# Mixer of a hybrid decoder layer: a step's instructions in another order on four queues

## What is computed

```
A  stick-breaking attention, 4 heads x 64      w = exp(z + suffix sums of log_sigmoid(-z)),  out = w @ v
B  gated delta rule, 4 heads x 128             m = strict_lower((k*beta) @ k^T * decay);  (1 + m)^-1 applied to values and keys
                                               v_new = u - w @ S;  o = (q*decay) @ S + (q @ k^T * decay) @ v_new
                                               S = S * chunk_decay + (k*decay)^T @ v_new
C  gated linear recurrence, 4 heads x 64       o = (q*exp(b)) @ S + scores(q, k, b) @ v;   S = exp(last)*S + (k*exp(last-b))^T @ v
mix = [rms(A)*gain, rms(B)*gain*silu(z), rms(C)*gain*sigmoid(g)];  x = x + mix @ w_out
x = x + (silu(h @ w_gate) * (h @ w_up)) @ w_down,  h = rms(x);   out = rms(x)
```

## Time and profile before

| | |
|---|---|
| TensorE busy | 1334.3 us, 96% of the span |
| DVE, ScalarE, POOL busy | 783.0, 591.8, 674.5 us |
| chain that ended last | PE 85%, DVE 4%, issue 4%, ACT 3%, POOL 2% |
| from 460 to 635 us, by windows of 25 us | TensorE busy 19.8 to 22.1 us, DVE 14.8 to 21.0, granted clock 0.86 to 0.93 |
| log_sigmoids (L1769), start and duration | 462.43: 0.42 us; 535.81: 1.10 us; 559.87: 1.11 us |
| softplus at 534.45 | three ACTIVATE, 1.33 us |
| out_high at 554.35 | 1.06 us |
| Exp of decays at 552.43 | 0.63 us |
| POOL's unit at 457.91, 128x256 | 0.71 us |
| two DVE products on update, 128x128, at 542.12 and 543.33 | 0.29 us each |

### The profile page before, as it was taken

The page is one execution under the profiler, slowest core; times in us unless marked ns, Lnnn a source line. Parts: engine busy times, 40 slices in busy tenths (PEclk is TensorE's granted clock), DMA queues, the critical chain, the costliest instruction groups (busy, mean ns, idle before and its releaser), DMA issues.

```text
span 1389.9 us, 24260 instructions
## 1 busy us (share of the span) xinstructions
PE 1334.3 (96%) x9101; PEld 1110.0 (80%) x9101; DVE 783.0 (56%) x1171; ACT 591.8 (43%) x1403; POOL 674.5 (49%) x583
## 2 busy tenths in 40 slices
PE   5999999999999888888999999999999999999997
PEld 4777887978888777777888788888888888788886
DVE  5014635557354588785147955555555556665657
ACT  6234535444343556552133433333333334344445
POOL 3233324143253577660210876766666777654442
PEclk9999999999999999898999999999999999999999
DMA  5131312423226333514210245444554545886663
GB/s 183 33 104 50 104 61 79 126 65 120 64 78 158 115 101 91 172 56 156 61 31 1 83 130 162 148 161 157 174 174 144 174 144 205 300 276 192 189 195 121
DMA packets 160371, 178.60 MB, mean 128 GB/s; under 512 B 9520, under 2 KB 110464, under 8 KB 160256
## 3 DMA queue, kind: packets, MB, share of 16 engines
q1 hardware_dynamic: 160112, 176.53, 40.1%
q10 hardware_dynamic: 144, 0.52, 0.1%
HBM read 124.32 MB, written 52.71 MB: 127 GB/s over the span
## 4 chain that ended last, share of the span: by engine, by line
PE 85%; DVE 4%; issue 4%; ACT 3%; POOL 2%; DMA 1%; SPq 0%; DVEq 0%; ACTq 0%; POOLq 0%
PE banks L2416 9%; PE banks L2417 9%; PE banks L2418 9%; PE banks L353 6%; PE banks L355 6%; PE banks L354 6%; PE banks L2427 4%; PE banks L2429 4%; PE banks L2428 4%; PE banks L692 2%; PE banks L693 2%; PE banks L694 2%; PE banks L2108 2%; PE banks L2110 2%; PE banks L2109 2%
## 5 line engine op out<-in xcount | busy, mean ns | idle before, releaser
L2574 POOL TENSOR_TENSOR w_l<-area,w_h 128x512 fp32r<-128x512 f32 x119 | 175.5, 1480 | 180.0 <-ACT w_h L2469 135.0
L2574 POOL TENSOR_TENSOR w_l<-w_raw,w_h 128x512 fp32r<-128x512 f32 x100 | 140.5, 1406 | 99.7 <-ACT w_h L2524 50.3
L353 PE MATMUL banks<-act_h,w_h 128*128 128x512 f32 x352 | 141.4, 402 | 0.0
L355 PE MATMUL banks<-act_h,w_l 128*128 128x512 f32 x352 | 137.5, 391 | 0.0
L354 PE MATMUL banks<-act_l,w_h 128*128 128x512 f32 x352 | 137.3, 390 | 0.0
L341 POOL TENSOR_TENSOR w_l<-w_raw,w_h 128x1024 fp32r<-128x1024 f32 x24 | 59.4, 2478 | 142.5 <-ACT w_h L334 125.3
L2416 PE MATMUL banks<-act_h,w_h 128*128 128x512 f32 x320 | 124.5, 389 | 0.0
L2417 PE MATMUL banks<-act_l,w_h 128*128 128x512 f32 x320 | 124.5, 389 | 0.0
L2418 PE MATMUL banks<-act_h,w_l 128*128 128x512 f32 x320 | 124.5, 389 | 0.0
L2427 PE MATMUL banks<-w_h,act_h 128*128 128x512 f32 x308 | 120.1, 390 | 0.3 <-DVE act_l L2726 0.3
L2428 PE MATMUL banks<-w_l,act_h 128*128 128x512 f32 x308 | 119.9, 389 | 0.0
(11 more groups left out here) (316 smaller groups left out, 3353.3 us busy)
## 6 DMA issues: line engine op xcount, KB each, us to landing
w_raw<-in_w_in SPq DMA_DIRECT2D x22, 512.0 KB, 4.1
w_raw<-in_w_gate SPq DMA_DIRECT2D x22, 512.0 KB, 4.6
area<-in_w_up SPq DMA_DIRECT2D x22, 512.0 KB, 4.8
ff_wide<-in_w_down SPq DMA_DIRECT2D x22, 512.0 KB, 4.4
down_sums<-ff_wide SPq DMA_DIRECT2D x11, 1024.0 KB, 4.1
area<-in_x SPq DMA_DIRECT2D x8, 1024.0 KB, 8.0
projected_tm<-area SPq DMA_DIRECT2D x32, 256.0 KB, 2.4
hidden_sums<-area SPq DMA_DIRECT2D x6, 1024.0 KB, 4.2
```

The costliest lines, as they stand in the source:

```text
L353: e.matmul(dst, w_h[:, b, k], act_h[:, k, cols], start=(k == 0), stop=False)
L355: mm = e.matmul(dst, w_l[:, b, k], act_h[:, k, cols], start=False, stop=(k == KT - 1))
L2574: e.tensor_tensor(slot(w_l, u), raw_use(u) if u < NU_FF else wd_raw(u - NU_FF), slot(w_h, u).bitcast(F32), ALU.subtract).then_inc(sems["fl ...
```

## The change

No instruction is added or taken away. These move within a step:

- TensorE: `key_key(v)` goes ahead of `gated_state(t)`.
- ScalarE: `decays` is split. Its first Exp (`decays`) goes behind `high(s, 1)`; the four Abs and the last Exp become `distances(v)` and go to the step's head. `softplus(u)` at the head becomes `softplus(v)` at the end of the step before. `inverse(u, 2)` goes ahead of `high(s, 0)`, `inverse(u, 4)` ahead of the last span.
- DVE: `log_sigmoids(u)` at the head becomes `log_sigmoids(v)` near the end of the step before. `final_sb(t)`, the scalings, become `final_sb(s)`, in the next step behind `gated_state(s)`. `update(u, 5)`, takes 6 and 7 go ahead of `new_state(t)`. `with_decay(v)` goes ahead of queries 2 and 3, and queries 4 to 6 go behind `update(v, 0)`, to the very end.
- SyncE and POOL keep their order.

```diff
 mixer_pe, step:
                 if live(u):
                     turn(u, 5)
                     pack(u, 6)
+                if live(v):
+                    key_key(v)
                 if live(t, NT - 1):
                     gated_state(t)
-                if live(v):
-                    key_key(v)
                 if live(t):
                     gated_out(t)
 mixer_act:
                 act(egr[:, :, :], gr[:, :, :], ACT.Exp, "egr")
+
+            def distances(c):
+                e.wait_ge(sems["gr_loaded"], 16 * (c + 1))
                 reach(e, "m", c)
                 reach(e, "at0", c)
                 for h in range(DNH):
 ...
 mixer_act, step:
                 if live(s):
                     gated_squares(s)
-                if live(u):
-                    softplus(u)
-                if live(s):
                     gated_lengths(s)
                 if live(u):
                     inverse(u, 0)
+                if live(v):
+                    distances(v)
                 if live(t):
                     new_values(t)
                 if live(u):
                     inverse(u, 1)
+                if live(u):
+                    inverse(u, 2)
                 if live(s):
                     high(s, 0)
 ...
                 if live(s):
                     high(s, 1)
-                if live(u):
+                if live(v):
+                    decays(v)
+                if live(u):
+                    inverse(u, 4)
                     spans(u, 3, 4)
-                    inverse(u, 4)
                 if live(t):
                     squares(t)
                     lengths(t)
-                if live(v):
-                    decays(v)
                 if live(t, NT - 1):
                     keys_turned(t)
                 if live(u):
                     inverse(u, 5)
                     whole_inverse(u)
+                if live(v):
+                    softplus(v)
                 if 0 <= t < 4:
                     out_high(e, 0, t)
 mixer_dve, step:
-                if live(u):
-                    log_sigmoids(u)
                 if live(t):
                     residual(t)
 ...
                 if live(s, NT - 1):
                     gated_state(s)
+                if live(s):
+                    final_sb(s)
                 if live(t):
                     take(t, 0)
 ...
                 if live(t):
-                    final_sb(t)
                     take(t, 4)
+                if live(u):
+                    pack(u, 5)
+                if live(t):
                     take(t, 5)
-                if live(u):
-                    pack(u, 5)
                 if live(s):
                     low(s, 1)
-                if live(t, NT - 1):
-                    new_state(t)
                 if live(u):
                     update(u, 5)
                 if live(t):
                     take(t, 6)
-                if live(u):
-                    queries(u, 2)
-                if live(t):
                     take(t, 7)
+                if live(t, NT - 1):
+                    new_state(t)
                 if live(u):
                     pack(u, 6)
-                    queries(u, 3)
                 if live(t):
                     final_dn(t)
 ...
-                if live(u):
-                    queries(u, 4)
-                    queries(u, 5)
-                    queries(u, 6)
                 if live(v):
                     with_decay(v)
+                if live(u):
+                    queries(u, 2)
+                    queries(u, 3)
+                if live(v):
+                    log_sigmoids(v)
                     scores(v)
                 if live(u):
                     update(u, 6)
                 if live(v):
                     update(v, 0)
+                if live(u):
+                    for lv in range(4, LEVELS):
+                        queries(u, lv)
```

More of the change, by code:

```diff
@@ L1660, in step @@
                     from_start(u)
-                if live(u):
-                    inverse(u, 2)
                     spans(u, 0, 3)
@@ L1690, in beside @@
                     decays(0)
+                    distances(0)
                 if unit == 1:
@@ L1706, in beside @@
                     decays(1)
+                    distances(1)
                     to_end(0)
@@ L1712, in mixer_act @@
             e.wait_ge(sems["zeroed"], 4)
+            softplus(1)
             for t in range(NT + 1):
@@ L1895, in step @@
                 if live(t):
-                    final_sb(t)
                     take(t, 4)
-                    take(t, 5)
                 if live(u):
                     pack(u, 5)
+                if live(t):
+                    take(t, 5)
                 if live(s):
                     low(s, 1)
-                if live(t, NT - 1):
-                    new_state(t)
                 if live(u):
@@ L1968, in mixer_dve @@
             e.wait_ge(sems["zeroed"], 4)
+            log_sigmoids(1)
             for t in range(NT + 1):
```

## The result

The changed kernel takes 1403.94 us (median of five executions, 1401.89 to 1414.82) against 1390.44 us: ratio 1.0106, 95% interval 1.0083 to 1.0129. It is slower by 13.5 us. The forecast was 1388.6 us, its range 1380.5 to 1396.5.

What follows compares the result with a forecast made beforehand. TensorE, busy 96% and in the mixer waiting mostly for DVE, was taken as the bound. Terms 2.5 - 7.1 - 0.8 + 2.45 + 1.0 = -1.95 us took the median 1390.61 to 1388.6 us, range 1380.5 to 1396.5.

Steps and rivals of the forecast that it cites:

- the dip at the head: Steps' start on TensorE: half clock after idling 1.7 to 3 us, +0.5 us a step (0 to +1.7); steps 1 to 3 25.0 each.
- the wait for the decay rows: Step 0, ScalarE: distances wait for rows landing 4.4 us after issue; 1.1 us arrive, making the step 25.6 us.
- Other moves cost nothing: Loads on SP: load_rest waits for the scalings, others queue behind it, all land before their first readers; no cost.
- steps 4 and 5: Mixer steps forecast at 23.15 + 0.45 = 23.6 us each, the 0.45 for a dip.
- The lock: DVE instructions with both inputs in SBUF stand still while POOL runs; queries 4 to 6 at the step's end wait.
- one sign: Sign of being right: one of the queries at the step's end takes over 1.5 us in steps 0 to 3.
- Key products directly behind take 7: Step's tail on TensorE: key products need only take 7, start at +15.7 instead of +17.56, at full clock.
- Step 6: Without the stalled scalings, the 3.10 us wait and most half clock go: 20.6 us, including 0.5 for a dip.
- The last step: Tile 7's transposes wait for scalings behind x: +2.45 us; a dip afterwards +1.0; step 7's first matmuls -0.8.
- the queries slip past POOL: Rival: queries 4 to 6 take the port before POOL, period near 23.1 us in all steps, 1380.5 us; chance 0.28.
- the transfer's bound: Rival: the channels' transfer, landing late ahead of softplus, bounds each step; 1398 us; chance 0.12.
- Nothing arrives: Rival: savings of steps 4 to 6 are kept down by dips at other places; 1393.5 us; chance 0.15.

Runs made afterwards that it cites:

- run 8: The changed kernel with two extra 128x512 matmuls ahead of key_state on TensorE in steps 1 to 6, filling the gap at the head: 1402.01 us, ratio 1.0069.
- run 4: The changed kernel with only tile 7's scalings back in step 7, ahead of take 4: 1405.48 us, ratio 1.0106.
- run 9: The changed kernel with tile 2's distances behind inverse 1 instead of ahead of new_values, in step 0 only: 1409.93 us, ratio 1.0117.
- run 12: run 10 with ScalarE's whole stream as before the change and log_sigmoids back at DVE's head: 1381.62 us, ratio 0.9922.
- run 7: The changed kernel with key_state's four matmuls issued five times in steps 1 to 6, filling TensorE's gap at the head: 1410.55 us, ratio 1.0137.
- run 3: The changed kernel with queries 4 to 6 back behind queries 3 and the scalings back ahead of take 4 of their own tile: 1379.38 us, ratio 0.9912.
- run 5: The kernel before the change, with only queries 4 to 6 moved to the very end of DVE's step: 1399.89 us, ratio 1.0066.
- run 1: The changed kernel with queries 4 to 6 back directly behind queries 3, ahead of scores: 1396.06 us, ratio 1.0037.
- run 6: The kernel before the change, with only the scalings moved to the next step's head behind gated_state: 1397.26 us, ratio 1.0038.
- run 11: run 10 with key_key back behind gated_state on TensorE: 1382.71 us, ratio 0.994.
- run 10: run 3 with tile 6's scalings kept in step 7's head and step 0's distances of tile 2 behind inverse 1: 1375.92 us, ratio 0.9899.

## Why the prediction was wrong

**The step that failed** is the price of TensorE's idle time at the head: "I put the dip at the head instead, where DVE hides most: +0.5 us a step, between 0 and +1.7." That price is one for dips as short as those of before, 3.4 us in most steps. In the changed kernel's steps 1 to 3 they lasted 13.6, 10.2 and 10.2 us and cost 3.7, 2.4 and 2.3 us, against 25.2 at full clock (run 8, which has the filler). Its steps 1 to 3 run the same instructions in runs 4 and 9; by the length of their half clock at the head, all taken together (us):

| half clock | none | 3.4 | 6.8 | 10.2 | 13.6 |
|---|---|---|---|---|---|
| steps of the changed kernel, runs 4 and 9 | | 25.1, 25.3 | 25.7 | 27.6, 27.5 | 28.9, 28.5, 28.6, 29.4 |
| steps of run 8 | 25.1, 25.2 | | | 27.6 | |

A dip of 3.4 us at the head is hidden, as I had it; one of 10 us is not. Nor does the place set the length: the waits ahead of all the steps in the first row are 2.1 to 3.1 us long. In the long ones DVE hides little: from 553 to 563 us TensorE is busy 9.96 of 10.00 us and DVE 5.38, so there DVE waits for TensorE. Steps 1 to 3 are 8.9 us over the forecast. 8.4 us are dips, where I had 1.5; the other 2.0 are that a step at full clock takes 25.2 us and not 24.5. In step 0 the half clock (20.5 us) comes on top of the wait for the decay rows, which was forecast:

```profile
467.24 1.28 ACT L1641 ACTIVATE area<-area,gc 128x128 f32<-128x128 f32 x4 [4.73 <-DMA area<-decay_rows]
```

With a wait as long (4.26 us) and 3.4 us of half clock, run 4 takes 25.7, as forecast; run 9, without the wait, 24.8. So of the 5.5 us over the forecast all but a tenth go with the dip of 17 us.

The Trainium skill (TensorE: Matmul & The Clock Gate, "HAM oscillation — how this bites in real kernels") sets the cost of half clock at half of its duration; by that a dip of 10.2 us would be, as an estimate, 5.1 us. In run 8 it was 2.4, in run 12 about 4: at full clock the same step has waits that the dip partly fills. The same section of the Trainium skill has idle gaps as the cause. The runs agree in that filling the gap took the dips from every head (run 7) and closing it left none in steps 2 to 5 (run 3); they don't show it gap by gap (runs 5 and 8), and run 1 has long dips although its heads have no gap.

**A second error: loads that I costed at nothing.** "Other moves cost nothing: load_rest waits for the scalings". SP's queue in step 4, of the changed kernel and, the same loads, of run 3:

```profile
583.23 0.32 SPq L1174 DMA_DIRECT2D area<-projected_tm  x1
583.61 0.41 SPq L657 DMA_DIRECT2D w_raw<-in_w_out  x1
584.13 0.60 SPq L1179 DMA_DIRECT2D area<-projected_cm  x1
585.45 0.36 SPq L1184 DMA_DIRECT2D area<-projected_cm  x1
```

```profile
575.07 0.32 SPq L1174 DMA_DIRECT2D area<-projected_tm  x1
575.44 0.42 SPq L657 DMA_DIRECT2D area<-in_w_out  x1
577.95 0.37 SPq L1179 DMA_DIRECT2D area<-projected_cm  x1
...
584.88 0.36 SPq L1184 DMA_DIRECT2D area<-projected_cm  x1
```

Four loads go out within 2.2 us where they were spread over ten. The DMA engines (busy tenths in 40 slices from 588 to 594 us; then a queue's packets, MB and share) are full until about 591 us:

```profile
DMA  9999999999999999997331100000000000000000
...
q8 instruction: 1, 0.02, 1.2%
```

and TensorE halts in the middle of a group whose operands are all there; the second row is a step later:

```profile
592.46 0.72 PE L1354 MATMUL banks<-area 128*128 128x128 f32 x5 [1.73 <-issue]
...
619.19 0.56 PE L1314 MATMUL banks<-area 64*64 64x32 f32 x19 [2.21 <-issue]
```

Such halts, one to four a kernel and 1.1 to 2.5 us long inside steps 1 to 6, are in the traces of all seven kernels with the scalings of every step at the head (the changed one, runs 1, 4, 6, 7, 8, 9); in those of the other seven there is none over 0.9 us. They fit a transfer of TensorE's own instructions queued behind the loads (its one packet in that stretch is the row above); no run moved the loads alone, so that is argued, not shown. In the changed kernel 6.8 us of half clock begin about 2 us behind each of the two. With the halts and half clock of 10 us in each (3.4 at the head, 6.8 there), steps 4 and 5 are 4.2 us over, each.

**Right, by their own steps.** The lock: queries 4 to 6 at 3.40 us in step 3 (I had 3.6, from +20.9 on; they begin at +24.2, and none takes over 1.5 us, as one sign had it: 1.39, 1.35 and 0.82); the scalings at the head at 1.04. A dip at the head that lasts 3.4 us: 25.1 and 25.3 for 25.0. Key products directly behind take 7, at full clock. The wait for the decay rows in step 0: about 1.0 us for 1.1. Step 6: 21.5 for 20.6, before 25.0. The last step, to which the earlier trace rows are the counterpart:

```profile
677.24 1.28 DVE L2125 TENSOR_TENSOR area<-area,banks 128x512 f32<-128x512 f32 x2 [6.22 <-DMA area<-in_x]
678.54 0.86 DVE L1840 SCALAR_TENSOR_TENSOR area<-banks,r_hg,area 128x64 f32<-128x64 f32 x4
679.32 0.86 DVE L1840 SCALAR_TENSOR_TENSOR area<-area,r_sb,gain_row 128x64 f32<-128x64 f32 x4
```

```profile
680.24 1.12 PE L1339 MATMUL banks<-ident,area 128*128 128x128 f32 x4 [3.26 <-DVE area L1840]
681.01 0.78 PE L2116 MATMUL banks<-w_h,act_h 128*128 128x512 f32 x1
```

The transposes wait 3.26 us for tile 7's scalings and the product starts 3.8 us behind the additions, 0.8 before. From step 7's residual to the span's end it is 758.1 us for 754.05: +4.0, where I had -0.8 + 2.45 + 1.0 = +2.65.

**The rivals.** That the queries slip past POOL did not come; nor did the transfer's bound: softplus waited for the channels 0.99 us in step 3, but run 3 keeps that chain and takes 22 us a step. "Nothing arrives" had the right mechanism, dips at other places, and far too small a price: 1393.5. The chance of 0.13 for slower was too low for a change whose likeliest course left TensorE idle by 1.7 to 3 us at the start of its serial stretch.

**The sum as measured.** Of the 23.8 us by which the profiled steps 0 to 6 exceed the forecast, 8.9 lie in steps 1 to 3 (6.9 for longer dips, 2.0 for longer steps), 5.5 are step 0's dip, 8.4 dips and halts of steps 4 and 5, 0.9 step 6's. Of the total, 11 us are what this execution took above the median. How much its dips are one execution's luck shows in run 4, where the same steps 0 to 6 take 180.0 us.

**Open.** What decides whether a gap is followed by half clock and for how long: 1.24 and 1.08 us in run 8, 1.83 us five times in run 5, 2.1 to 3.1 us in the table above had unlike sequels. And how the 4.2 us of each of steps 4 and 5 divide between halts and dips; by run 7 a halt of 1.4 us at full clock is worth about 1.6 us.

## What to carry to other kernels

Price an idle gap on TensorE by the longest half clock that may follow it, not by the last one seen. Behind like gaps it lasted 3.4 to 13.6 us; at the head those of 3.4 us cost 0.1 us at most and those of 10 us and more 2.3 to 4.3, where the gaps were 2.1 to 3.1. A place with independent products is no shelter: in run 11 steps with 3.4 us of half clock under the tail's products were 1.1 to 2.6 us longer than the one without. Put instructions with two SBUF inputs where POOL is idle and nobody waits, and never last before the instruction that releases TensorE: with three queries and four scalings left at home the rest of this change is worth 11.4 us (1379.4 against 1390.8), and 14.5 with run 10's two further edits (1375.9 against 1390.5). When an instruction moves later, look at which loads are released by it and whether they now go out together.

## What the runs showed beyond that

- Repairs to one step of the changed kernel did not show in the total: runs 4 and 9 mended their step by 3 us and, with the dip that went, by 6, and the totals were 1405.5 and 1409.9 where the changed kernel has 1403.9, all within each other's intervals. Run 3, which closes the gap at every head, keeps its gain.
- The spread differs with the order: run 1's executions lie 17 us apart, the changed kernel's 13, run 3's 0.5. That long dips come and go between executions would explain it; only one execution of each kernel has a trace, so it is not shown.
- Three queries behind `update(v, 0)` take 3.40 us beside out_low and causal, 1.97 in run 5, where out_low ended before, and five of them 1.10 where POOL is idle.
